# Decode attention of a hybrid decoder step: from alternating key and value phases to one uniform loop over pairs of pages

## The reference, cut to what matters

```python
def diff_attend(q, k, v, q_pos, k_pos, lam, slopes):
    s = jnp.einsum("bqhmd,bkhmd->bhmqk", q, k, preferred_element_type=jnp.float32) * (HEAD_DIM_A ** -0.5)
    dist = q_pos[:, None] - k_pos[None, :]
    bias = -slopes[:, None, None] * dist.astype(jnp.float32)[None]
    s = jnp.where((dist >= 0)[None, None, None], s + bias[None, :, None], -jnp.inf)
    p = jax.nn.softmax(s, axis=-1)
    a = p[:, :, 0] - lam * p[:, :, 1]
    return jnp.einsum("bhqk,bkhd->bqhd", a.astype(v.dtype), v)
```

## Time and profile before

| What | Value |
|---|---|
| Median of 3 runs | 4206.64 us (4204.91 to 4207.31) |
| Span of the profiled execution | 4207.0 us |
| TensorE busy over the span | 91% |
| VectorE, ScalarE busy | 48%, 30% |
| GpSimd busy | 19.6 us in all |

### The profile page before, as it was taken

How to read it: one execution, slowest core, us unless ns; L and a number is a source line. 1 busy time by engine, 2 the same in 40 slices (tenths; PEclk the granted TensorE clock), 3 DMA queues, 4 the chain that set the end, 5 groups by cost and what they waited for, 6 DMA issues and landing times. The chain is left out here.

```text
span 4207.0 us, 69193 instructions
## 1 busy us (share of the span) xinstructions
PE 3810.4 (91%) x27044; PEld 3486.2 (83%) x27044; DVE 2026.5 (48%) x2676; ACT 1247.3 (30%) x1514; POOL 19.6 (0%) x50
## 2 busy tenths in 40 slices
PE   5999996675786999999996998999999999999998
PEld 4999995454676777777673896999999999999998
DVE  5222222693536888788886425333333333333333
ACT  2111111242104666666664212112121211212121
POOL 0000000000000000000000000000000000000000
PEclk8999998887968999999998998999999999999999
DMA  5443431315446887888885312222322222222221
GB/s 146 107 112 104 114 102 68 123 39 179 89 148 224 272 269 274 285 277 279 285 296 182 114 50 80 82 89 80 90 80 88 82 83 86 80 89 80 90 80 62
DMA packets 459389, 574.18 MB, mean 136 GB/s; under 512 B 38150, under 2 KB 333108, under 8 KB 458156
## 3 DMA queue, kind: packets, MB, share of 16 engines
q1 hardware_dynamic: 459260, 572.54, 43.5%
HBM read 521.68 MB, written 50.80 MB: 136 GB/s over the span
## 5 line engine op out<-in xcount | busy, mean ns | idle before, releaser
L64 PE MATMUL f_acc<-xf_hi,ffn_lo 128*128 128x280 f32 x2048 | 600.1, 293 | 16.5 <-DVE xf_lo L229 16.5
L64 PE MATMUL f_acc<-hidden_hi,ffn_lo 128*128 128x280 f32 x2048 | 600.3, 293 | 10.8 <-DVE hidden_lo L2298 10.8
L66 PE MATMUL f_acc<-xf_hi,ffn_hi 128*128 128x280 f32 x2048 | 600.7, 293 | 0.0
L65 PE MATMUL f_acc<-xf_lo,ffn_hi 128*128 128x280 f32 x2048 | 599.0, 292 | 0.0
L65 PE MATMUL f_acc<-hidden_lo,ffn_hi 128*128 128x280 f32 x2048 | 597.4, 292 | 0.0
L66 PE MATMUL f_acc<-hidden_hi,ffn_hi 128*128 128x280 f32 x2048 | 596.2, 291 | 0.0
L64 PE MATMUL z_acc<-xn_hi,win_lo 128*128 128x280 f32 x1536 | 451.4, 294 | 19.0 <-DVE xn_lo L229 19.0
L66 PE MATMUL z_acc<-xn_hi,win_hi 128*128 128x280 f32 x1536 | 451.2, 294 | 0.0
L65 PE MATMUL z_acc<-xn_lo,win_hi 128*128 128x280 f32 x1536 | 449.9, 293 | 0.0
L2267 ACT ACTIVATE ffn_hi<-ffn_raw 128x2048 fp32r<-128x2048 f32 x128 | 244.2, 1908 | 670.6 <-PE f_acc L66 634.4
L64 PEld LDWEIGHTS f_acc<-xf_hi,ffn_lo 128*128 128x128 f32 x2048 | 387.6, 189 | 21.7 <-issue 11.1
(11 more groups left out here) (325 smaller groups left out, 6317.6 us busy)
## 6 DMA issues: line engine op xcount, KB each, us to landing
dc_pages<-in_cache_k SPq DMA_DIRECT2D x256, 512.0 KB, 4.6
dc_pages<-in_cache_v SPq DMA_DIRECT2D x256, 512.0 KB, 5.2
ffn_raw<-in_w_up SPq DMA_DIRECT2D x64, 1024.0 KB, 6.4
ffn_raw<-in_w_down SPq DMA_DIRECT2D x64, 1024.0 KB, 5.0
win_raw<-in_w_in SPq DMA_DIRECT2D x48, 1024.0 KB, 6.3
wout_raw<-in_w_out SPq DMA_DIRECT2D x16, 1024.0 KB, 6.3
z_scratch<-z_out SPq DMA_DIRECT2D x48, 280.0 KB, 2.4
sm_c<-in_state_C SPq DMA_DIRECT2D x32, 256.0 KB, 4.8
```

Source lines behind the costliest of these rows:

```text
L64: nc.tensor.matmul(out, wlo, xhi, start=first, stop=False)
L65: nc.tensor.matmul(out, whi, xlo, start=False, stop=False)
L66: return nc.tensor.matmul(out, whi, xhi, start=False, stop=last)
```

## The change

The key and value phases become one loop over **slots**. Slot s turns key pair s, makes the scores of pair s-1 and multiplies the values of pair s-7. Four slots make a **unit** (a chunk of 8 pages); each unit has a softmax of its own with its own maximum, and `factors`, `factors_end`, `double`, `mixers` and `combine` bring the four units of a sample together. The main differences:

```diff
-    RING = 8
-    PIECES = 4
+    CP = 8
+    CHUNKS = PG // CP
+    KEYS = CP * P
+    UNITS, PAIRS, PPU = NB * CHUNKS, NP // 2, CP // 2
+    RING, VBUF = 4, 3
+    LAG = PPU + 3
+    SLOTS = PAIRS + LAG
-        pk = [ps(f"dc_pk{i}", [P, 1024]) for i in range(2)]
-        pscore = [ps(f"dc_pscore{i}", [P, 512]) for i in range(2)]
+        pk = [ps(f"dc_pk{i}", [P, 512]) for i in range(2)]
+        pscore = ps("dc_pscore", [P, 512])
...
+            for m in range(NP):
+                pool.wait_ge(vhi, m + 1)
+                G.tensor_tensor(vl[:, m % VBUF, :], vring[:, m % RING, :], vh[:, m % VBUF, :].bitcast(F32),
+                                ALU.subtract).then_inc(vlo, 1)
...
+            for s in range(SLOTS + 2):
+                v = pair_of(s)
+                for i in range(2):
+                    if s < PAIRS:
+                        turn(s, i, 0)
+                        turn(s, i, 1)
+                    if 0 <= v < PAIRS:
+                        values(v, i)
+                    if i == 0:
+                        u, at = s // PPU - 1, s % PPU
+                        if 2 <= at and 0 <= u < UNITS:
+                            turn_p(u, at - 2, s)
...
+                if 1 <= s <= PAIRS:
+                    scores(s - 1)
...
+                v = pair_of(s)
+                if 0 <= v < PAIRS and v % PPU == PPU - 1:
+                    keep(v // PPU)
+                if 1 <= s <= PAIRS:
+                    take(s - 1)
+                    top(s - 1)
```

More of the change, by code:

```diff
@@ L1568, in decode_attention @@
+        own_split = sems("dc_own_split")
         pages = [x[0].rearrange("n p h e -> n p (h e)") for x in (a["cache_k"], a["cache_v"])]
+        pair_of = lambda s: s - LAG
+        last_of_sample = lambda u: u % CHUNKS == CHUNKS - 1
         block = ctx.enter_context(nc.Block())
[L1572 to L1587, removed]
@@ L1717, in pe_v @@
                 for half in range(2):
                     cs = slice(half * 512, half * 512 + 512)
-                    mm = exact_passes(nc, pout[0:R, cs], ph[s][:, p, :], pl[s][:, p, :], vslot(kh, p)[:, cs],
-                                      vslot(kl, p)[:, cs], p == 0, False)
-                mm.then_inc(valued, 1)
-                if following is not None and p == TURN_AT:
-                    pe_turn(pe, following, 1 - s, following + 1)
-            pe.wait_ge(own_out, b + 1)
-            for half in range(2):
-                cs = slice(half * 512, half * 512 + 512)
-                mm = nc.tensor.matmul(pout[0:R, cs], pown[s][:, :], vown[:, cs], start=False, stop=True)
@@ new lines, in values @@
+                    if not x:
+                        mm = nc.tensor.matmul(pout[0:R, cs], php[:, u % 2, x, 0:R], vl[:, m % VBUF, cs], start=False,
+                                              stop=False)
+                mm.then_inc(valued, 1)
+                if final and last_of_sample(u):
+                    for half in range(2):
+                        cs = slice(half * 512, half * 512 + 512)
+                        nc.tensor.matmul(pout[0:R, cs], pown[:, 0:R], vownl[:, cs], start=False, stop=False)
+                        mm = nc.tensor.matmul(pout[:, cs], pown[:, :], vownh[:, cs], start=False, stop=True)
+                    mm.then_inc(valued, 1)
@@ new lines, in double, with combine @@
+            def double(b, s):
+                pe.wait_ge(factored, b + 1)
+                pe.wait_ge(biased, min(s - 1, PAIRS))
+                pe.wait_ge(plo, 2 * CHUNKS * (b + 1))
+                nc.tensor.matmul(pscore[:, 0:CHUNKS], twice[:, :], fac[:, :], start=True, stop=True).then_inc(doubled, 1)
+            def combine(b, s):
+                pe.wait_ge(mixed, 2 * b + 2)
+                pe.wait_ge(kept_one, CHUNKS * b + CHUNKS)
+                pe.wait_ge(biased, min(s - 1, PAIRS))
+                for i in range(CHUNKS):
+                    mm = nc.tensor.matmul(pscore[:, 0:TS], kept[:, b % 2, i, :], mixer[:, i, :], start=(i == 0),
+                                          stop=(i == CHUNKS - 1))
+                mm.then_inc(combined, 1)
@@ L1868, in _, with mixers @@
+            def mixers(b):
+                dve.wait_ge(doubled, b + 1)
+                if b >= 1:
+                    dve.wait_ge(combined, b)
+                V.tensor_copy(factor[:, :], pscore[:, 0:CHUNKS]).then_inc(mixed, 1)
+                dve.wait_ge(mixed, 2 * b + 1)
+                for i in range(CHUNKS):
+                    ins = V.tensor_scalar(mixer[:, i, :], comb[:, :], factor[:, i:i + 1], None, ALU.mult)
+                ins.then_inc(mixed, 1)
             dve.wait_ge(lined, LINED)
```

704 lines of the change are left out of this document (348 added, 356 removed).

## The result

The changed kernel takes 4264.8 us (median of 4 runs, 4262.0 to 4267.1) against 4205.8 us before (4201.1 to 4207.3): a ratio of 1.0139, 95% interval 1.0125 to 1.0154. The prediction said 4168 and faster, with 4250 as its upper end; it was wrong.

The account below looks back on a forecast made before the run. TensorE bounds the kernel before, a chain of waits through all engines after. Stage terms 15 + 837 + 35 + 31 + 4 + 34 = 956 us against 994.7, so 4168 from 4207.0, range 4130 to 4250.

Parts of the forecast that it names:

- D: Time from a slot's first transpose until VectorE can begin the first half page: 1.5 us, 0.42 of it the addition.
- the first rival: A chain of waits through all engines sets each slot's length: 4168 us, from 4135 to 4195, chance 0.46.
- Rival 3: VectorE's addition (L1807), reading two SBUF tiles, waits for GpSimd's instruction: 49 us and 5 more, 4222, chance 0.33.
- slot 2: Third slot of a unit of four: 6.3 us; folding comes first at its end, so the addition is not held.
- The clock at nothing: TensorE's clock was costed at nothing, with the longest gap in a slot put at about 1.7 us.
- It shows as idle time between L1796 and L1807: Sign of Rival 3 in the profile: VectorE idle between these lines until GpSimd's instruction ends.
- The chain, L = D + 4.81: Length of a slot, first transpose to end of scores: D plus 4.81 us, 6.3 us without special work.
- slot 3: Last slot of a unit of four: 8.4 us, with D at 3.55 after the folding.
- rival 2: TensorE's own work still sets the loop's pace, 6.0 to 6.3 us a slot: 4081 us, chance 0.07.
- GpSimd's price: GpSimd's subtraction for a page of values: taken as 2.2 us, bounds 1.1 and 3.7, no cost up to about 2.9.
- Rival 4: GpSimd itself takes 3 us or more a page of values: 4175 to 4219 us, chance 0.14.
- Transfers at nothing: Loading four pages, 2.1 MB, in 6.9 us (304 GB/s) was costed at nothing.

Follow-up runs that it names:

- filler: The changed kernel with small matmuls on constants, into an unread PSUM tile, where TensorE waits: 4237.8 us, ratio 1.0071.
- both_in_psum: The changed kernel with the slow part of the scores and the mixers' input in PSUM instead of SBUF: 4172.5 us, ratio 0.9909.
- low_on_vector: The changed kernel with the values' low parts back on VectorE and GpSimd idle: 4278.0 us, ratio 1.0160.
- six_matmuls: both_in_psum with the stacking of the probabilities undone for six of a chunk's eight pages: 4235.7 us, ratio 1.0067.
- bank_lay: bank with the two copies of the next queries on ScalarE instead of VectorE: 4188.5 us, ratio 0.9944.
- bank: both_in_psum with a PSUM bank apart from the scores for turned probabilities, doubled factors and combined output: 4201.2 us, ratio 0.9981.
- gpsimd_halves: The changed kernel with each GpSimd subtraction of 1024 columns cut into two of 512: 4223.3 us, ratio 1.0031.

## Why the prediction was wrong

- **The step that failed** is the 0.42 us for the addition in D, that is, the choice of the first rival (0.46) over the third (0.33). The trace of before could not decide it: no two engines there read SBUF in this way. Rival 3's mechanism, place and sign were right, down to slot 2, where the folding comes first and the addition takes 0.42 us. The Trainium skill ("SBUF — State Buffer", section "Who interferes with whom") said it outright for the addition with two SBUF inputs, and of the copies and the tensor-by-scalar operations that they can contend; the runs agree on all three (1048, 1066 and 1078 ns where 413, 171 and 244 are free), and they agree that a reduction is not held (L1815, 411 ns).
- **Its price was too low too**: 49 us for the addition and 5 for small operations, 4222 in all. (Its three holds add up to 2.0 us a unit, 60 over the loop; the prediction counts 1.6 of them and doesn't show why.) Measured: 67 (4264.8 to 4197.8) and 25 (4197.8 to 4172.5). In the unit above the holds are 1.6, 1.4, 1.7 and 0 us, where 0.4, 0.4, 1.2 and 0 stood: GpSimd does both pages of a slot in one run of 4.74 us, which in the first case begins 3.8 us into the slot (1699.10 to 1702.90) and ends 2.4 after it, not 1.1. The mixers alone, held up to four in a row, were 27 of VectorE's us (32 x (1078 - 244) ns).
- **The clock at nothing**: wrong, 27 us (`filler`), most of it inside those 92: `filler` has 7 windows below 0.75, `both_in_psum` 32, the changed kernel 127. I had the longest gap at 1.7 us; the held additions make it 2.0 to 2.3. What waits bring a fall I can't say: in `low_on_vector` none is longer than 1.62 us, and the clock is 0.92 all the same.
- **It shows as idle time between L1796 and L1807**: wrong, the record of L1807 is longer.
- **The chain, L = D + 4.81**: right, once the addition and the mixers are free: the stage takes 955.2 us against a sum of 956, the program 4172.5 against 4168, a unit 27.9 against 27.7, TensorE waits 0.6 us a slot for the keys' low parts and 1.60 + 0.61 in slot 3. The 3.3 us of folding ahead of the addition are real as well: with 2.0 of them moved, 34 us go. That the sum comes out within 1 us is luck in part: the loop of 121 slots took 860 us where 837 and 34 of the samples' own work stood, and what comes behind it 45 where 35 stood. (D after the folding adds up to 3.67 from its own terms, not 3.55, 4 us over the loop.)
- **TensorE sets the pace (rival 2)**: no. But `six_matmuls` shows that its work on the first page counts in part, which a chain of one path does not have.
- **GpSimd's price**: 2.2 taken, 2.39 measured, inside the bounds of 1.1 and 3.7; two thirds busy in the stage of `both_in_psum`. The Trainium skill's figure ("GPSIMD Engine Reference", section 3.1), halved, gave an estimate of 2.25, which is 6% under the trace. Rival 4 is out: it stays under 2.9.
- **Transfers at nothing**: right, TensorE waited 1.0 us for pages of keys.

The three parts, then: 1057.5 us of stage in the changed kernel are the predicted 956, 92 us of holds and of the clock behind them (the clock 27 at most), and 9 that stages, counted in single profiles, leave over. Not settled are the last 16 us of `bank_lay`: that the joined waits and the clock behind them cost this is read from the trace, not tried alone.

## What to carry to other kernels

Before work goes to GpSimd, list what VectorE runs beside it with its operands in SBUF, small operations too, and give each one operand in PSUM, or another engine, or a place where GpSimd is idle; halves on GpSimd gave back 41 of the 92 us, where no PSUM is free. Count a held operation to the end of the GpSimd instruction that runs when it starts, and several in a row once each; look for them as a mean that is too long for their size, not as idle time. And price TensorE's waits at more than themselves: a fall of the clock behind them cost some 1.5 us in a slot here, and falls came behind waits of 2.0 to 2.3 us and behind shorter ones.

## What I had not expected of the hardware

- GpSimd's subtraction of 128x1024 took 2389 ns and that of 128x512 1304: 2.1 ns a column and 0.22 us for each instruction.
- VectorE's copy of 64x32, 0.17 us, took up to 2.3 us in `bank`; whether it is held depends on where it falls beside GpSimd, so that an edit elsewhere (the bank) moved the time by 13 us through the copies alone.
- It goes the other way too: where VectorE's addition started 0.08 us before GpSimd's subtraction of 128x512 (`gpsimd_halves`), the subtraction took 1489 ns, against 1292 at the median.
- 1,100 useless matmuls made the kernel 27 us faster, by clock alone.
- 2.2 to 2.7 us of waiting in the last slot of a unit went with a clock below 1.00 in 6 of 22 such slots where it came in two pieces (`both_in_psum`), and 2.3 us of it in one piece in 13 of 17 (`bank_lay`).
